# Weights laid out in transfer units, front modulation chunks that pair shift and scale, and vectors that arrive as columns

## Time and profile before

| | |
|---|---|
| median of 3 runs | 2022.6 us (2022.3 to 2022.95) |
| span of the profiled execution, first to last instruction | 2020.7 us |
| what the median has beyond that span | 1.9 us |
| PE busy | 1988.9 us, 98% of the span |
| DVE, ACT, POOL busy | 65%, 42%, 3% |
| moved by DMA | 319.19 MB, 158 GB/s on average |

### The profile page before, as it was taken

How to read it: one execution, slowest core, us unless ns; L and a number is a source line. 1 busy time by engine, 2 the same in 40 slices (tenths; PEclk the granted TensorE clock), 3 DMA queues, 4 the chain that set the end, 5 groups by cost and what they waited for, 6 DMA issues and landing times.

```text
span 2020.7 us, 25508 instructions
## 1 busy us (share of the span) xinstructions
PE 1988.9 (98%) x10263; PEld 1654.0 (82%) x10263; DVE 1322.7 (65%) x1642; ACT 857.5 (42%) x1007; POOL 68.4 (3%) x121
## 2 busy tenths in 40 slices
PE   8999999999999999999999999999999999999998
PEld 5878778778888888877778888899888888988887
DVE  5886979556555354576776565766866577678565
ACT  5332332224322222446665554554544356445442
POOL 0000000010111000000000000000000000000000
PEclk9999999999999999999999999999999999999999
DMA  9544444252554343332137555545655554546552
GB/s 357 184 151 136 144 148 145 84 167 74 172 155 158 104 151 126 102 113 84 53 103 219 168 177 177 188 165 170 216 194 193 176 172 162 196 157 218 189 190 81
DMA packets 250759, 319.19 MB, mean 158 GB/s; under 512 B 10113, under 2 KB 166066, under 8 KB 250130
## 3 DMA queue, kind: packets, MB, share of 16 engines
q1 hardware_dynamic: 235152, 262.77, 40.2%
q0 software_dynamic: 14416, 53.14, 7.8%
q10 hardware_dynamic: 1074, 1.66, 0.2%
HBM read 316.48 MB, written 1.05 MB: 157 GB/s over the span
## 4 chain that ended last, share of the span: by engine, by line
PE 86%; DVE 6%; ACT 2%; DVEq 2%; DMA 1%; issue 1%; ACTq 1%; SPq 0%
PE ps L2326 14%; PE ps L2327 14%; PE ps L2321 8%; PE ps L2881 6%; PE ps L3142 6%; PE ps L2340 5%; PE ps L2336 5%; PE ps L2337 5%; PE ps L2798 3%; PE ps L2269 3%; PE ps L3145 3%; PE ps L2406 2%; PE ps L2887 2%; PE ps L2891 2%; PE ps L2888 2%; PE ps L2801 2%
## 5 line engine op out<-in xcount | busy, mean ns | idle before, releaser
L1241 DVE TENSOR_TENSOR w_lo<-raw,w_hi 128x2048 fp32r<-128x2048 f32 (+1 forms) x244 | 553.0, 2271 | 239.1 <-ACT w_hi L609 238.3
L609 ACT ACTIVATE w_hi<-raw 128x2048 fp32r<-128x2048 f32 (+1 forms) x244 | 462.0, 1897 | 254.3 <-PE ps L2321 149.6
L2326 PE MATMUL ps<-w_hi,big_hi 128*128 128x512 f32 x760 | 298.8, 393 | 0.9 <-DVE big_lo L1739 0.7
L2327 PE MATMUL ps<-w_hi,big_lo 128*128 128x512 f32 x760 | 296.2, 390 | 0.0
L2336 PE MATMUL ps<-hT_hi,w_hi 128*128 128x512 f32 (+1 forms) x512 | 192.4, 380 | 1.9 <-issue 1.0
L2337 PE MATMUL ps<-hT_lo,w_hi 128*128 128x512 f32 (+1 forms) x512 | 190.3, 376 | 0.0
L2326 PE MATMUL ps<-w_hi,hT_hi 128*128 128x512 f32 x416 | 167.7, 403 | 4.6 <-DVE hT_lo L1246 4.6
L2326 PEld LDWEIGHTS ps<-w_hi,big_hi 128*128 128x128 f32 x760 | 142.8, 188 | 30.4 <-issue 1.0
L2327 PEld LDWEIGHTS ps<-w_hi,big_lo 128*128 128x128 f32 x760 | 142.9, 188 | 28.9 <-issue 0.5
L2327 PE MATMUL ps<-w_hi,hT_lo 128*128 128x512 f32 x416 | 163.2, 392 | 0.0
L3142 PE MATMUL ps<-h_both,w_hi 128*128 128x512 f32 x512 | 128.0, 392 | 0.0
(11 more groups left out here) (314 smaller groups left out, 3027.4 us busy)
## 6 DMA issues: line engine op xcount, KB each, us to landing
raw<-ffn_w_in SPq DMA_DIRECT2D x88, 512.0 KB, 5.1
raw<-w_in SPq DMA_DIRECT2D x80, 512.0 KB, 4.6
raw<-w_up SPq DMA_DIRECT2D x64, 512.0 KB, 4.7
raw<-w_down SPq DMA_DIRECT2D x64, 512.0 KB, 4.5
raw<-ret_w_in SPq DMA_DIRECT2D x48, 512.0 KB, 5.4
front<-ada_w POOLq DMA_DIRECT2D x24, 1024.0 KB, 5.5
raw<-ffn_w_out SPq DMA_DIRECT2D x40, 512.0 KB, 4.5
raw<-ada_w POOLq DMA_DIRECT2D x64, 256.0 KB, 4.3
```

Of the source, the lines that this page charges most:

```text
L609: act.activation(SPLIT_HI[PAIR_OF[u]][:, 0:m], raw[:, RAW_OF[u], 0:m], ACT.Copy).then_inc(sem["hi_ready"], 1)
L1241: op(SPLIT_LO[PAIR_OF[u]][:, 0:m], raw[:, RAW_OF[u], 0:m], SPLIT_HI[PAIR_OF[u]][:, 0:m].bitcast(F32), ALU.subtract).then_inc(sem["lo_ready ...
L2326: pe.matmul(out, x[0][:, t * P:(t + 1) * P], w, start=start, stop=False)
L2327: pe.matmul(out, x[1][:, t * P:(t + 1) * P], w, start=False, stop=False)
```

## The change

All changes are in the order and the layout of work; the arithmetic of the result is the same.

1. The host packs every unit in the layout of its slot, 8 KB in a row per partition. `load` is one DMA transfer of 1 MB for each unit instead of two of 512 KB. The four helpers are gone.
2. `ada_w` is packed too. A front chunk `j` holds shift and scale of the same 256 features, and comes as two transfers of 1 MB with 8 KB rows. The later chunks (`EXTRA`) keep their contents.
3. The small vectors are one host array `columns`; ACT loads three parts of it straight into `cols`, and the identity, in four transfers. The PE turns and DVE copies of them are gone.
4. SP's order is x, context, `qa0`, chunks 0, 1, 2, `qb0`, chunk 3, then all units. All eight halves of the front are on SP's queue, none on ACT's, and POOL no longer fetches the context.
5. The context is normalised and turned right behind the latent tokens. The row copy out of PSUM moves from DVE to ACT, and applying shift and scale moves from ACT to DVE (`modulated`), block by block for both token sets; splitting is per block of 512 tokens.
6. PE's order is by block (`first_high`, `first_low`), with the chunks between, and `awake` is moved and has other sizes.

```diff
@@ sync
-                for j in range(2):
-                    sp.dma_start(view(raw[:, r, 0:n], j), part(j)).then_inc(unit_in[r], 16)
+                    sp.dma_start(raw[:, r, 0:m], A["units"][u, :, 0:m]).then_inc(unit_in[r], 16)
...
-            sp.dma_start(const[:, 0:P], A["table"][:, 0:P]).then_inc(sem["ident_in"], 16)
+                for h in range(2):
+                    sp.dma_start(FRONT_IN[2 * j + h], A["ada"][j, :, 4 * h:4 * h + 4, :]).then_inc(front_in[2 * j + h], 16)
             sp.dma_start(X4[:, 0:2, :], token_rows(A["x"][0])).then_inc(sem["x_in"], 16)
+            sp.dma_start(X4[:, 2:4, :], token_rows(A["ctx"][0])).then_inc(sem["xc_in"], 16)
+            load(FIRST_END["qa0"])
             modulation(0)
-            sp.dma_start(FRONT_IN[3][:, 2:4, :], kpn(A["ada_w"][0])[:, 6:8, FRONT[1] * 512:(FRONT[1] + 1) * 512]).then_inc(front_in[3], 16)
-            part(w, 0, 0, RH * RDK)
+            modulation(1)
             modulation(2)
+            load(FIRST_END["qb0"])
             modulation(3)
-            part(w, 4, 0, RH * RDK)
...
+            load(TOTAL_UNITS)
@@ gpsimd
-            pool.wait_ge(front_in[3], 32)
-            fetch(X4[:, 2:4, :], token_rows(A["ctx"][0]), sem["xc_in"])
-            pool.wait_ge(sem["front_used"], 2)
+            pool.wait_ge(sem["front_used"], 1)
             fetch(dec[:, 0, :], bcast(A["ret_decay_logit"].rearrange("a b c -> a (b c)"), 8), sem["dec_in"])
...
             pool.wait_ge(sem["front_used"], 4)
@@ scalar
+            act.dma_start(cols[:, V_C:V_NG], A["columns"][:, V_C:V_NG]).then_inc(sem["c_in"], 16)
+            act.dma_start(ident, A["table"][:, C_IDENT:C_IDENT + P]).then_inc(sem["ident_in"], 16)
+            act.dma_start(cols[:, 0:V_C], A["columns"][:, 0:V_C]).then_inc(sem["vec_in"], 16)
+            act.dma_start(cols[:, V_NG:161], A["columns"][:, V_NG:161]).then_inc(sem["vec_in"], 16)
...
+            def row(b, a, n):
+                act.wait_ge(sem["front_used"], n)
+                act.activation(at(a, 512), bank(b), ACT.Copy).then_inc(sem["row_ready"], 1)
+            first_squares(0)
+            first_root(0)
+            first_squares(1)
+            first_root(1)
+            for t in range(4):
+                turned_x(t)
             split(FIRST_END["qa0"])
-            act.drain()
-            act.wait_ge(sem["mod_ready"], 2)
-            modulate(0, 0, 1, 0, 0, lambda c: XTL[:, c, :])
-            first_norm(1)
+            row(0, 8960, 1)
+            row(1, 9472, 2)
             act.wait_ge(sem["dec_abs"], s.next("dec_abs"))
             act.activation(dec[:, 2, :], dec[:, 1, :], ACT.Exp, scale=-1.0).then_inc(sem["dec_exp"], 1)
-            turned_x(2)
-            turned_x(3)
-            act.drain()
-            modulate(0, 0, 1, 1, 0, lambda c: XTC[:, c, :])
+            row(0, 8960, 3)
             split(FIRST_END["qb0"])
-            act.wait_ge(sem["mod_ready"], 4)
-            modulate(0, 0, 1, 0, 4, lambda c: XTL[:, c, :])
-            modulate(0, 0, 1, 1, 4, lambda c: XTC[:, c, :])
+            row(1, 9472, 4)
@@ vector
+            def mod_cols(b, j):
+                dve.wait_ge(sem["at_full"], s.next("at_full"))
+                for g in (0, 8):
...
+                    dve.tensor_reduce(m, parts, AX.X, ALU.add)
+                drain()
+                for g in (0, 8):
...
+                    i = op(m, m, cols[:, c:c + 2].unsqueeze(2).to_broadcast([P, 2, 2]), ALU.add)
+                i.then_inc(sem["mod_ready"], 1)
+                drain()
+            def modulated(c):
+                xm = at(4096 + 512 * c, 2, 256)
+                for m, x in enumerate((XTL, XTC)):
+                    ts(xm[:, m, :], x[:, c, :], mod[:, 0, 8 + c, m:m + 1], mod[:, 0, c, m:m + 1], ALU.mult, ALU.add)
+                drain()
+                dve.tensor_copy(hT_hi[:, c, :], at(4096 + 512 * c, 512))
+                drain()
+                lo(hT_lo[:, c, :], at(4096 + 512 * c, 512), hT_hi[:, c, :]).then_inc(sem["h_part"], 1)
+            first_norm(0)
+            first_norm(1)
+            dve.wait_ge(sem["xt_read"], 4)
+            mod_cols(2, 0)
+            modulated(0)
+            modulated(1)
             split(FIRST_END["qa0"])
+            mod_cols(3, 1)
+            modulated(2)
+            modulated(3)
             dve.wait_ge(sem["dec_in"], s.next("dec_in", 16))
             dve.scalar_tensor_tensor(out=dec[:, 1, :], in0=x, scalar=-1.0, in1=x, op0=ALU.mult, op1=ALU.max).then_inc(sem["dec_abs"], 1)
-            first_norm(1)
+            mod_cols(2, 2)
+            modulated(4)
+            modulated(5)
+            split(FIRST_END["qb0"])
             decay_start()
             series(15, 13, 11, 9)
+            mod_cols(3, 3)
+            modulated(6)
+            modulated(7)
             decay_end()
@@ tensor
+            pe.wait_ge(sem["ones_set"], 1)
+            awake(24)
+            pe.wait_ge(sem["ident_in"], 16)
             x_turned(0)
             x_turned(1)
+            awake(8)
             x_turned(2)
             x_turned(3)
+            pe.wait_ge(sem["silu_c"], 1)
+            chunk(0, 0)
+            awake(4)
+            to_cols(2, 8960)
+            awake(8)
+            first_high("qa0", 0)
+            first_high("qa0", 1)
+            chunk(1, 1)
+            first_low("qa0", 0)
+            to_cols(3, 9472)
+            first_low("qa0", 1)
             chunk(2, 0)
+            first_high("qa0", 2)
+            to_cols(2, 8960)
+            first_high("qa0", 3)
+            first_low("qa0", 2)
+            used(first_low("qa0", 3))
             chunk(3, 1)
+            first_high("qb0", 4)
             to_cols(3, 9472)
+            first_high("qb0", 5)
+            first_low("qb0", 4)
+            first_low("qb0", 5)
+            first_high("qb0", 6)
+            first_high("qb0", 7)
+            first_low("qb0", 6)
+            used(first_low("qb0", 7))
```

More of the change, by code:

```diff
@@ L383, in _ @@
             s = Side()
-            def load(view, n, part):
-                u = s.loaded
-                assert n == SIZES[u], (u, n, SIZES[u])
-                r = RAW_OF[u]
-                v = RAW_BEFORE[u]
-                if v is not None:
-                    sp.wait_ge(sem["lo_ready"], v + 1)
-                for j in range(2):
-                    sp.dma_start(view(raw[:, r, 0:n], j), part(j)).then_inc(unit_in[r], 16)
-                s.loaded += 1
-            def by_k(w, k0, nk, c0, n):
-                b = [0, nk // 2, nk]
-                load(lambda d, j: d.rearrange("p (k n) -> p k n", k=nk)[:, b[j]:b[j + 1], :], nk * n,
-                     lambda j: kpn(w)[:, k0 + b[j]:k0 + b[j + 1], c0:c0 + n])
@@ L414, in modulation, with load @@
-            def modulation(j):
-                for k0 in (0, 4):
-                    f = 2 * j + k0 // 4
-                    for k in (0, 2):
-                        sp.dma_start(FRONT_IN[f][:, k:k + 2, :], kpn(A["ada_w"][0])[:, k0 + k:k0 + k + 2, FRONT[j] * 512:(FRONT[j] + 1) * 512]).then_inc(front_in[f], 16)
-            w = A["ret_w_in"][0]
+            def load(n):
+                while s.loaded < n:
+                    u = s.loaded
+                    r, v, m = RAW_OF[u], RAW_BEFORE[u], SIZES[u]
+                    if v is not None:
+                        sp.wait_ge(sem["lo_ready"], v + 1)
+                    sp.dma_start(raw[:, r, 0:m], A["units"][u, :, 0:m]).then_inc(unit_in[r], 16)
+                    s.loaded += 1
@@ L522, in _ @@
-            for i in range(2):
-                layer(i)
-            assert s.loaded == TOTAL_UNITS
+            load(TOTAL_UNITS)
             for t in range(2):
@@ L2341, in feature, with awake @@
                 return i
[L2343 removed]
+            def awake(n):
                 for _ in range(n):
[L2346 to L2353 removed]
@@ L2363, in x_turned, with first_high @@
                 i.then_inc(sem["xt_full"], 1)
-            def half(j, b, h):
-                pe.wait_ge(front_in[2 * j + h], 32)
-                return sums(b, FRONT_IN[2 * j + h], 4 * h)
-            awake(4, SZ_FLAT)
-            half(0, 0, 0)
-            pe.wait_ge(sem["cols_read"], 1)
+            def first_high(name, k):
+                w = unit(name, 4)
+                pe.wait_ge(sem["h_part"], k + 1)
+                for t in range(4):
+                    high(bank(4 + t), hT(k), t, w[0][:, k % 4, :], k == 0)
@@ L2372, in _, with first_low @@
+            def first_low(name, k):
+                w = unit(name, 4)
+                lows(name)
+                for t in range(4):
+                    i = pe.matmul(bank(4 + t), hT(k)[0][:, t * P:(t + 1) * P], w[1][:, k % 4, :], start=False, stop=(k == KD - 1))
+                return i
+            pe.wait_ge(sem["ones_set"], 1)
+            awake(24)
+            pe.wait_ge(sem["ident_in"], 16)
             x_turned(0)
             x_turned(1)
-            half(0, 0, 1).then_inc(sem["front_used"], 1)
@@ new lines, in laid_out @@
+def laid_out(I):
+    import numpy as np
+    f = np.float32
```

(13 more changed lines are left out.)

297 lines of the change are left out of this document (115 added, 182 removed).

## The result

The changed kernel takes **2031.7 us**, the median of 4 runs (2031.4 to 2032.43), against 2022.49 us of the kernel before in 4 runs on the same chip: ratio 1.0046, 95% interval 1.0035 to 1.0058. It is slower by 9.2 us. I had said 2023.0, with 2027.2 as the upper end: wrong, and outside the range. The span of the profiled execution is 2029.7 us, 9.0 more than before.

What follows compares the result with a forecast made beforehand. PE's and DVE's chains end nearly together at the turns of q and k; DVE's later head 0 start was to bind. +0.65 and -0.2 for units, rounded +0.4, on 2020.7 plus 1.9 gave 2023.0 us; range 2018.5 to 2027.2.

Steps and rivals of the forecast that it cites:

- The failed step: Front: no work after x waits for a transfer, so merged transfers and longer rows cost and give nothing there.
- The walk: Front in its new order, timed by earlier durations: DVE begins head 0 at 50.1, turns of q and k move +0.65 us.
- rival 3: Front: PE's clock falls before `first_high` 0 and 1, +4.5 us on DVE's chain, 2027.2 us; chance 0.12.
- rival 4: Front: hand-offs, rows, `modulated` and a late later piece at their upper bounds, +2.5 us, 2025.5 us; chance 0.10.
- `modulated`: DVE's front: two new operations with the drain take 0.55 us, 1.65 us a block, block 0 ready at 23.0.
- What bounds the front: DVE's start on its head 0 list, 41.2 us of work, sets the turns; PE's 3.4 us earlier end is lost.
- Rival 1: Front: DVE does not bind and PE's gain goes through, -3.4 and -0.2 us, 2019.0 or 2018.5 us; chance 0.10.
- a bar: Head 0: the first later modulation piece lands at 48.6, holding DVE to about a microsecond before its present time.
- The units: After the front: one transfer per unit gives -0.2 us, bounds 0 and 16.0 us.
- Rival 2: After the front: a third of PE's 16.0 us idle hangs on late units, -5.3 us, 2017.7 us; chance 0.07.
- longer rows give nothing by themselves: Transfers: longer rows do nothing for the speed of a transfer; inside the forecast, which has chance 0.61.
- The signs I had named: Wrong if DVE starts head 0 before 47 or after 53, PE turns without waiting, or later PE idle changes over 1 us.

Runs made afterwards that it cites:

- experiment 1: Changed kernel with DVE's wait for the small vectors and three operations on them moved behind both norms: 2025.41 us, ratio 1.0017.
- experiment 4: Changed kernel with 50 awake products at the start in place of 24, DVE's wait left in place: 2030.54 us, ratio 1.0039.
- experiment 5: On experiment 1, 24 DVE summing operations of the first four later modulation pieces left out: 2023.62 us, one run.
- experiment 6: On experiment 1, decay value fetched early, its exponential and series done in ACT's and DVE's waits, first later piece fetched after two chunks: 2023.83 us, ratio 1.0007.
- experiment 7: On experiment 6, ACT applies shift and scale to the context half of each block, PE sums chunk 1 ahead of `first_high` 0: 2020.92 us, ratio 0.9994.
- experiment 9: On experiment 8, chunk 0 fetched ahead of `qa0`, ACT's split later, chunk 1 halved around `first_high` 0, last row turned earlier: 2019.81 us, ratio 0.9988.
- experiment 3: Changed kernel with its three column transfers made one: 2026.08 us, ratio 1.0017; with the two late ones each cut in half instead: 2036.26 us, one run.
- experiment 8: On experiment 7, 32 awake products, columns in one transfer, chunk 1 behind `first_high` 0, chunk 3 two steps sooner: 2021.84 us, ratio 0.9998.
- experiment 10: Kernel before with only the units packed by the host, one transfer each: all units 2022.36 us, ratio 1.0001; all but the first two 2022.08 us, ratio 0.9997.
- experiment 2: Changed kernel with the two later column transfers on SP's queue ahead of x in place of ACT's: 2026.53 us, one run.
- the first of 10: Kernel before with every unit packed by the host and loaded in one transfer: 2022.36 us (2020.8 to 2023.91), ratio 1.0001.
- the second of 10: Kernel before with units 2 to the last packed by the host, one transfer each, front untouched: 2022.08 us (2021.49 to 2022.36), ratio 0.9997.

## Why the prediction was wrong

**The failed step** is the sentence "Nothing on the walk after x waits for a transfer". One thing did: DVE, for the columns, ahead of its first norm. The walk gave the root at 9.7 from ACT's times alone; it asked of ACT only whether it had issued its transfers ("ACT issues 4 transfers in place of 11, so it is ready"), not when they land and who stands behind them. The changed part of DVE's list has the wait in its first line, in front of `first_norm`, and the prediction costs neither the wait nor what is queued behind it: the root came at 14.73, and in experiment 1, without that wait, at 9.80. Worth, by experiments 1 and 4: 6.3 us in time, of which 1.2 are the clock and 5.1 the wait. At the turns of q and k, ahead of experiment 4's longer wait for a unit, the clock is 2.0 of 7.2 us.

**The clock (rival 3).** The mechanism was right, the place was not. I looked for it before `first_high`, where the clock was 1.00. It fell twice elsewhere: in the 6.5 us pause at 9.4 to 15.9, and behind PE's pause before `g00`. That pause I had forecast at 2.0 us; it was 2.69, with the clock at 0.50 in 66 to 68 us, and I gave it no price. On PE's own chain it costs 1.7 us: in experiment 5, where PE then has no wait, it takes 36.1 us from `g00` to the turns in place of 34.5. In the changed kernel it cost nothing, since DVE set the turns: in experiment 4 the clock stayed up there, and PE waited that much longer for DVE. The rival's own sum had a slip, 2023.0 + 4.5 is 2027.5 and not 2027.2; the measured time is beyond both.

**The ring (rival 4).** With the wait out of the way the walk can be checked term by term against experiment 1. `modulated` was mis-sized: 1.92 us from block to block and not 1.65, since its two operations with the drain take 0.81 and not 0.55.

```profile
21.28 0.74 DVE L1247 TENSOR_SCALAR arena<-arena,mod 128x256 f32<-128x256 f32 x2
22.09 0.43 DVE L1249 CAST hT_hi<-arena 128x512 fp32r<-128x512 f32 x1
22.59 0.69 DVE L1122 TENSOR_TENSOR hT_lo<-arena,hT_hi 128x512 fp32r<-128x512 f32 x1
23.20 0.73 DVE L1247 TENSOR_SCALAR arena<-arena,mod 128x256 f32<-128x256 f32 x2
```

Seven of the eight blocks stand on the chain to head 0, since PE works through block 0 while DVE makes block 1: 1.9 us at 0.27 each, most of the difference between the 50.1 of the walk and the 52.30 of experiment 1. The rest of the walk held: first columns, rows, decay operations and chunks within a few tenths. So even without the wait the turns would have moved by 3.3 us and not by 0.65, and the 2025.41 us of experiment 1 are this rival's 2025.5, though from another term: it gave `modulated` 0.15 a block and the rest to rows, hand-offs and a late piece.

**What bounds the front** was right. Rival 1 (DVE does not bind) is refuted: experiment 5 takes work from DVE's list and PE's wait at the turns goes; experiments 6, 7 and 9 begin the list 2.1, 4.5 and 5.9 us sooner than experiment 1 and move the turns by 2.1, 4.8 and 6.1. What I had not seen is how much could be had there. The walk had a bar against it, the first piece of the later modulation, and that bar is there: with one transfer for the columns (experiment 3) DVE waited 0.80 us for this piece. Experiments 6 to 9 fetch it two chunks sooner and get past it.

**The units** (-0.2): the profiles bear out the sign. The stretch from the turns to the end is 0.2 and 0.7 us shorter with the units alone, and ACT's wait near 1063 us 0.9 to 1.1 us. The times do not show it: both ratios of experiment 10 take in 1. Rival 2 (5.3 us) is refuted by experiment 10. That longer rows give nothing by themselves was shown for the units alone; the layout of `ada_w` was never tried apart from the rest. In the changed kernel PE waits for no chunk, but in experiments 6 to 9, with a shorter front, it waits 0.67 to 1.50 us for one.

**The signs I had named.** I had written that I am wrong "if DVE starts head 0 before 47 or after 53 us"; it started at 59.46. The pauses before `g00` and before the turns were there, and PE's idle time behind the turns changed by less than 1 us.

The sum of the parts: 5.1 for the wait, 1.2 for the clock behind it, 3.4 for DVE's list (experiment 1 against the kernel before; what is regained later is inside it) make 9.7, against 9.2 measured. The kernel before was itself 0.5 us faster on the chip of experiment 1, which is all of the difference: the parts are differences of the same times, so their sum is no test of them.

## What to carry to other kernels

When a change reorders an engine's list, write down for each engine the first wait of the new list, when its event can come, and what stands behind it that does not need it. Put a wait as late as its first user. Count small transfers beside a queue of large ones by their number, not by their bytes: join them, or put them first. And where PE's chain is the one that ends last, price a pause of 2.7 us or more twice: once for the pause, and once for the clock behind it (1.7 us here).

## What the runs showed of the hardware

- Transfers of 128 rows on ACT's queue, beside 1 MB transfers with 8 KB rows on SP's, land 2.7 us apart whether they carry 8 or 64 KB: 5.9, 8.7, 11.5, 14.0 us; the last at 19.5 with two more, all columns at 6.7 with one. Whether the number of transfers or that of rows decides was not separated. Ahead of the large ones (experiment 2) the columns are there at 3.8.
- Some 4 us behind the issue of a 4 KB fetch of POOL (8 values to each of 128 partitions) all queues together move 225 to 279 GB/s in a window of 2 us, and 376 to 426 in the window before it, in the changed kernel and in experiments 1 and 6; in experiment 4 it is 336. That the fetch is the cause was not tested apart; the fall moves with it.
- Long rows load at 417 to 421 GB/s from 5 to 25 us, against 365 to 408 with rows of 1 and 2 KB; in the time of the kernel no run shows a gain from this.
- Behind pauses of PE of 2.90, 3.12 and 6.51 us, and of 4.63 us in the kernel before, the granted clock was 0.50 for some microseconds; behind 1.30, 1.46, 2.22 and 2.42 us it stayed at 1.00. Of the pauses before `g00`, 2.67 to 2.70 us long, it fell behind those of the changed kernel and of experiments 1, 2, 3 and 5 and stayed at 1.00 in experiment 4.
- The same kernel can differ by 3 us from run to run (experiments 6 and 7, the first of 10), where another stays within 0.9 (the second of 10).
